# Moving the activation tiles against the weight buffers, modulo 512 bytes, stage by stage

## The reference

```
block 0:  proj = rmsnorm(x) @ nsa_w_in            # sparse attention, then memory attention
          x += concat(mix, cross) @ w_o[0]        # (256x1024) @ (1024x1024)        "wo0"
          x += swiglu(rmsnorm(x))                 # 1024 -> 2 x 2816 -> 1024        "f0"
block 1:  the same with the RWKV-7 recurrence as mixer; "wo1", "f1"
          x = rmsnorm(x)
block 2:  proj = rmsnorm(x) @ w_in_2              # spatial gating and forgetting attention
          x += rmsnorm(merged @ w_out_2)          # "wo2"
          x += rmsnorm(swiglu(rmsnorm(x)))        # "f2"
swiglu(h) = (silu(h @ w_gate) * (h @ w_up)) @ w_down     # hidden width 2816
```

## Time and profile before

| | us |
|---|---|
| median of 3 runs (1283.18 to 1285.41) | 1285.11 |
| the profiled execution | 1282.11 |
| its span, first to last instruction | 1280.3 |
| TensorE busy | 1204.6 (94%) |
| VectorE busy | 759.6 (59%) |
| ScalarE busy | 595.4 (47%) |
| mean granted TensorE clock | 0.966 |

### The profile page before, as it was taken

One profiled execution on the slowest core, in us unless ns is written; L12 is line 12 of the kernel. 1 busy time (PEld: TensorE's weight loads), 2 busy tenths in 40 slices (PEclk: granted clock), 3 DMA queues, 4 the chain that ended last, 5 costly groups with the idle time before them and its releaser, 6 DMA issues.

```text
span 1280.3 us, 24099 instructions
## 1 busy us (share of the span) xinstructions
PE 1204.6 (94%) x10320; PEld 1109.7 (87%) x10320; DVE 759.6 (59%) x1289; ACT 595.4 (47%) x1003; POOL 38.8 (3%) x44
## 2 busy tenths in 40 slices
PE   5999989999999998799799999999989988999997
PEld 4999878999988877798489999889988986999985
DVE  5555646666646677634566666465744575666644
ACT  4666545444435642232344444354328655444433
POOL 0000000000000102331000000000000000000000
PEclk9999989999999979899799999999989998999999
DMA  9822124867555431000259665537544343676651
GB/s 271 237 87 83 67 67 116 224 183 197 183 188 154 152 99 66 2 4 3 67 149 262 188 177 196 197 104 226 179 151 124 108 161 103 168 195 185 180 195 66
DMA packets 222693, 184.50 MB, mean 144 GB/s; under 512 B 19394, under 2 KB 208080, under 8 KB 222460
## 3 DMA queue, kind: packets, MB, share of 16 engines
q1 hardware_dynamic: 221386, 181.50, 47.6%
q10 hardware_dynamic: 1202, 1.47, 0.3%
HBM read 181.90 MB, written 1.05 MB: 143 GB/s over the span
## 4 chain that ended last, share of the span: by engine, by line
PE 83%; DVE 10%; ACT 4%; issue 1%; SPq 1%; DMA 1%; DVEq 0%; ACTq 0%
PE bank L776 23%; PE bank L777 22%; PE bank L778 22%; DVE w_lo L2027 2%; PE bank L1055 2%; PE bank L1273 1%; ACT w_hi L1580 1%; PE bank L1039 1%; PE bank L1249 1%; DMA ring<-in_nsa_w_in 1%; PE bank L1257 1%; PE bank L919 1%; SPq L713 1%; PE bank L923 1%; DVE act_lo L1997 1%
## 5 line engine op out<-in xcount | busy, mean ns | idle before, releaser
L2027 DVE TENSOR_TENSOR w_lo<-ring,w_hi 128x1024 fp32r<-128x1024 f32 x326 | 383.1, 1216 | 264.8 <-ACT w_hi L1580 264.6
L1580 ACT ACTIVATE w_hi<-ring 128x1024 fp32r<-128x1024 f32 x326 | 323.4, 1041 | 425.9 <-PE bank L778 407.4
L776 PE MATMUL bank<-act_hi,w_hi 128*128 128x256 f32 (+1 forms) x1512 | 428.0, 283 | 6.1 <-issue 3.4
L777 PE MATMUL bank<-act_lo,w_hi 128*128 128x256 f32 (+1 forms) x1512 | 424.6, 281 | 0.0
L778 PE MATMUL bank<-act_hi,w_lo 128*128 128x256 f32 (+1 forms) x1512 | 424.1, 280 | 0.0
L776 PEld LDWEIGHTS bank<-act_hi,w_hi 128*128 128x128 f32 (+1 forms) x1512 | 284.7, 188 | 10.7 <-issue 6.7
L777 PEld LDWEIGHTS bank<-act_lo,w_hi 128*128 128x128 f32 (+1 forms) x1512 | 284.6, 188 | 0.3
L778 PEld LDWEIGHTS bank<-act_hi,w_lo 128*128 128x128 f32 (+1 forms) x1512 | 283.9, 188 | 0.3
L776 PE MATMUL bank<-w_hi,act_hi 128*128 128x256 f32 (+1 forms) x448 | 141.0, 315 | 8.5 <-DVE act_lo L2503 4.2
L777 PE MATMUL bank<-w_lo,act_hi 128*128 128x256 f32 (+1 forms) x448 | 138.9, 310 | 0.0
L778 PE MATMUL bank<-w_hi,act_lo 128*128 128x256 f32 (+1 forms) x448 | 138.5, 309 | 0.0
(11 more groups left out here) (312 smaller groups left out, 1292.1 us busy)
## 6 DMA issues: line engine op xcount, KB each, us to landing
ring<-in_w_ffn_in SPq DMA_DIRECT2D x88, 512.0 KB, 5.2
ring<-in_w_in SPq DMA_DIRECT2D x28, 1024.0 KB, 5.3
ring<-in_w_ffn_out SPq DMA_DIRECT2D x22, 1024.0 KB, 4.9
ring<-in_rw_w_in SPq DMA_DIRECT2D x11, 1024.0 KB, 5.3
ring<-in_w_gate SPq DMA_DIRECT2D x22, 512.0 KB, 4.0
ring<-in_w_up SPq DMA_DIRECT2D x22, 512.0 KB, 5.2
ring<-in_w_down SPq DMA_DIRECT2D x11, 1024.0 KB, 4.9
ring<-in_w_o SPq DMA_DIRECT2D x8, 1024.0 KB, 4.9
```

Source lines behind the costliest of these rows:

```text
L776: pe.matmul(o, ahl[0], bhl[0], start=first, stop=False)
L777: pe.matmul(o, ahl[0], bhl[1], start=False, stop=False)
L1580: act.activation(w_hi[:, (m % SPLITS) * SLOT + lo:(m % SPLITS) * SLOT + hi], ring[:, r * SLOT + lo:r * SLOT + hi], copy).then_inc(tick(own ...
L2027: dve.tensor_tensor(w_lo[:, c], ring[:, r * SLOT + lo:r * SLOT + hi], w_hi[:, c].bitcast(F32), ALU.subtract).then_inc(tick(own, "lo_ready" ...
```

## The change

`act_hi` and `act_lo` become one region `act_pair` with 64 columns of room at its end. `home(shift)` gives the pair of views that begins `shift` columns further, and each stage has a shift of its own. `SHARED` is rounded up so that the arena lies at the same place modulo 512 bytes as the start of the region. `tt` moves with the home of `wo1`.

| stage | shift, columns | bytes past the weights' place | before |
|---|---|---|---|
| all others (`fm`) | 16 | 64 | 64 |
| `wo0` | 0 | 0 | 64 |
| `f0` | 8 | 32 | 64 |
| `wo1` | 48 | 192 | 64 |
| `f1` | 32 | 128 | 64 |
| `wo2` | 32 | 128 | 64 |
| `f2` | 64 | 256 | 64 |

```diff
-    act_hi = place("act_hi", KT * S, dtype=F32R)
-    ACT_LO = fixed_at[0]
-    act_lo = place("act_lo", KT * S, dtype=F32R)
+    LINE, ROOM, MIX1_HOME = 128, 64, 48
+    ACT_HI = fixed_at[0]
+    act_pair = place("act_pair", 2 * KT * S + ROOM, dtype=F32R)
+    ACT_LO = ACT_HI + KT * S
...
+    fixed_at[0] += (ACT_HI - fixed_at[0]) % LINE
     SHARED = fixed_at[0]
...
-    fm = (tiles(act_hi), tiles(act_lo))
+    def home(shift):
+
+        return tuple(tiles(act_pair[:, i * KT * S + shift:(i + 1) * KT * S + shift]) for i in range(2))
+
+    fm = home(16)
+    fm_of = {"wo0": home(0), "f0": home(8), "wo1": home(MIX1_HOME), "f1": home(32), "wo2": home(32), "f2": home(ROOM)}
...
-    tt = place("tt", 2 * H * CH, ACT_LO - SHARED).rearrange("p (r u t) -> p r u t", r=2, u=H)
+    tt = place("tt", 2 * H * CH, ACT_LO + MIX1_HOME - SHARED).rearrange("p (r u t) -> p r u t", r=2, u=H)
...
-                fm_unit(f"{tag}_in{j}", fm)
+                fm_unit(f"{tag}_in{j}", fm_of[tag])
...
-            row_unit("wo0_", j, 4, fm)
+            row_unit("wo0_", j, 4, fm_of["wo0"])
...
-        from_banks([(fm, lambda k: ("norm2", k))])
+        from_banks([(fm_of["f0"], lambda k: ("norm2", k))])
```

More of the change, by code:

```diff
@@ L1425, in _ @@
                 pe.wait_ge(sem("mix1_lo"), j + 1)
-            row_unit("wo1_", j, 4, fm)
+            row_unit("wo1_", j, 4, fm_of["wo1"])
         residual_to_fm(4, lambda i: evacuated("wo1_0", i))
@@ L1490, in _ @@
         for j in range(4):
-            row_unit("wo2_", j, 4, fm)
+            row_unit("wo2_", j, 4, fm_of["wo2"])
         residual_to_fm(4, lambda i: (sem("post_added"), i + 1))
@@ L1752, in _ @@
             step_end(s)
-        from_banks([(fm, None)])
+        from_banks([(fm_of["wo0"], None)])
         rows_ahead("wo0")
@@ L1799, in _ @@
         act.wait_ge(*filled("crT"))
-        act.activation(fm[0][:, 6:8, :], two("crT"), copy).then_inc(tick(own, "cross_hi"), 1)
+        act.activation(fm_of["wo1"][0][:, 6:8, :], two("crT"), copy).then_inc(tick(own, "cross_hi"), 1)
         def act_hop(hop, c):
@@ L1839, in _ @@
             act.wait_ge(sem("mix1_ready"), j + 1)
-            act.activation(fm[0][:, 2 * j:2 * j + 2, :], mix_fm[:, 2 * j:2 * j + 2, :], copy).then_inc(tick(own, "mix1_hi"), 1)
+            act.activation(fm_of["wo1"][0][:, 2 * j:2 * j + 2, :], mix_fm[:, 2 * j:2 * j + 2, :], copy).then_inc(tick(own, "mix1_hi"), 1)
         rows_ahead("wo1")
@@ L1843, in _ @@
         squares(4, x_tm)
-        from_banks([(fm, lambda k: ("norm2", 8 + k))])
+        from_banks([(fm_of["f1"], lambda k: ("norm2", 8 + k))])
         ahead("wo1_3")
@@ L1902, in _ @@
         ahead("gb3")
-        from_banks([(fm, None)])
+        from_banks([(fm_of["wo2"], None)])
         rows_ahead("wo2")
@@ L1907, in _ @@
         squares(8, x_tm)
-        from_banks([(fm, lambda k: ("ffn_pre_g_2", k))])
+        from_banks([(fm_of["f2"], lambda k: ("ffn_pre_g_2", k))])
         ahead("wo2_3")
@@ L2416, in _ @@
         dve.wait_ge(sem("cross_hi"), 1)
-        dve.tensor_tensor(fm[1][:, 6:8, :], two("crT"), fm[0][:, 6:8, :].bitcast(F32),
+        dve.tensor_tensor(fm_of["wo1"][1][:, 6:8, :], two("crT"), fm_of["wo1"][0][:, 6:8, :].bitcast(F32),
                           ALU.subtract).then_inc(freed(own, "crT"), 1)
@@ L2502, in _ @@
             ts = slice(2 * j, 2 * j + 2)
-            dve.tensor_tensor(fm[1][:, ts, :], mix_fm[:, ts, :], fm[0][:, ts, :].bitcast(F32),
+            dve.tensor_tensor(fm_of["wo1"][1][:, ts, :], mix_fm[:, ts, :], fm_of["wo1"][0][:, ts, :].bitcast(F32),
                               ALU.subtract).then_inc(tick(own, "mix1_lo"), 1)
```

## The result

The changed kernel takes 1286.5 us (median of 20 runs, 1283.0 to 1292.7), the kernel before 1280.1 us (20 runs, 1272.0 to 1289.7). The ratio is 1.0051, with a 95% interval of 1.0033 to 1.0069: slower by half a percent, where 1270 us and a gain were forecast. The stated range, 1251 to 1290, holds the time; the direction was the other one.

The account below looks back on a forecast made before the run. TensorE, busy 94% of the span, was taken as the bound through its matmul steps. 14.3 + 1.8 less about 0.6 gave 15.5 us off 1282.1, so 1266.6; plus 3.0 made 1269.6, stated as 1270, range 1251 to 1290.

Parts of the forecast that it names:

- What bounds the kernel, and what to read: Whole kernel: TensorE busy 94% of the span; the start-to-start matmul step counts, read from start times or window counts.
- First feed-forward products: f0, f1, f2: 3168 matmuls of 256 columns would step at 113.3 ns in place of 117.8, 14.3 us less.
- a sign of being wrong: Homes of f1 and f2: the prediction is wrong if 128 and 256 bytes are worse places than 64; no size given.
- the slow rival: f0, f1, f2 go to 120 ns or beyond: 1292 us at 120, 1313 at 127; chance 0.20.
- Two levels at one place: Matmuls with 256 columns: two stable levels, near 118 and 113 ns, can occur at one place, as in `sv0`.
- The other sign of being wrong: Feed-forward stages: the prediction is wrong if the level depends on how a stage is entered; no size given.
- Output projections: `wo0`, `wo1`, `wo2`, 96 matmuls of 512 columns each: 0.6 us less for each, 1.8 us in all.
- The rest of TensorE: 3456 matmuls and transposes outside `product`, whose operands move against each other: taken as 0, plus or minus 2 us.
- 510 to 630 us as long as now: The 120 us around the recurrence, holding 2418 matmuls and transposes, were to last as long as before.
- VectorE, ScalarE, weights in time: Splits and weight loads: no loss, 0 us; weights arrive in time; ScalarE's wait per unit falls from 3.03 to about 2.8 us.
- Nothing gives the gain back: Feed-forward units: 2.2 us of slack for the splits, of which a faster unit takes 0.2; loads keep up.
- The base: Starting time: profiled execution 1282.1 us, with 3.0 us added because the median of the runs shown was 1285.1.

Follow-up runs that it names:

- the second look: The changed kernel, unedited, profiled once more in a later set, where it took 1286.46 us, ratio 1.0034 to the kernel before.
- `f2_at_112`: Changed kernel with only the home of f2 moved, from 256 to 112 bytes: 1279.55 us, ratio 0.9975 to the kernel before.
- `all16`: Changed kernel with every home back at 64 bytes, in the new layout: 1282.4 us, ratio 1.0015 to the kernel before.
- `all16_same`: Changed kernel with every home at 64 bytes, timed again on one chip beside the changed kernel: 1286.23 us, ratio 1.0034 to the kernel before.
- `f28`: Changed kernel with f0, f1 and f2 at 112 bytes and all other homes at 64: 1272.6 us, ratio 0.9926 to the kernel before.
- `three_places`: Changed kernel with f0 at 0, f1 at 192 and f2 at 80 bytes, all other homes at 64: 1287.5 us in one look.
- `after`: First profiled look at the changed kernel, unedited; span 1282.2 us, median of its timed runs 1286.5 us.
- `best`: Changed kernel with f0, f1, f2 and projections of blocks 0 and 1 at 112 bytes, output projections at 0, block 2's projections at 64: 1266.2 us, ratio 0.9882 to the kernel before.

## Why the prediction was wrong, by its own steps

**What bounds the kernel, and what to read.** Right: the time is in the steps of the matmuls, and they follow the place. Each step was read from a count in a window, and the isolated matmul confirmed them to 0.1 ns. By the Trainium skill, "TensorE: Matmul & The Clock Gate", section "Step-by-step: what each phase is for", TensorE's two read ports are independent, loading the next weights takes no read bandwidth from the running matmul, and the step is the columns at 2.4 GHz plus about 2.5 ns. The isolated matmul, with nothing else at work, shows 113.3 to 120.0 ns by place where that gives 109, so for this form the trace does not agree.

**First feed-forward products: this is the step that failed.** It put f0, f1 and f2 at 113.3 ns, 14.3 us less, because two of the homes are farther from the weights' place than any in the trace and "a small push may be enough" to reach the lower level. They came to 116.6, 118.7 and 120.0: 1056 x (-1.1 + 0.6 + 2.3) / 1000 = +1.9 us. (In the second look f0 stayed at 117.8, which makes about +3 us.) The place is not a distance along which the loss shrinks. It repeats every 256 bytes, so f2's 256 bytes are the weights' own place again, whose 120 ns stood in the earlier trace rows. Modulo 512 was the diff's unit, and the prediction took it over without a row. The prediction named as a sign of being wrong that 128 and 256 bytes are worse places than 64, and they are. Where the low level came every time (30 isolated visits, 368 bytes included, and seven stages of the kernel) is 112 bytes, a place that neither kernel used. The bounds were right (113.2 to 120 ns holds all of it), and the slow rival named 120 ns and gave 1292, with a chance of 0.20; it came true for f2 alone, and the mean step of the three, 118.4 ns, stays under the 118.6 from which that rival was to decide. That the time went its way is partly luck: these steps are 1.9 us of the measured 6.4.

**Two levels at one place.** Right as a fact: f0 of the kernel before had 118 in three looks and 113 in one. But it was weighed too heavily: 3 of 24 isolated visits and 1 of 23 stages at 64 bytes. The rows it was read from, `sv0` and `fv`, are of another form, activations stationary, and forms have different rows. The other sign of being wrong, that the level depends on how a stage is entered, also came true: at 192 bytes a wait changed it. What in an entry chooses the level stays open.

**Output projections.** Right in sign, and `wo0` in size, by the very row it was taken from: 0.6, 0.4 and 0.1 us less, 1.1 in place of 1.8. `wo1` and `wo2` had no row. Their lower levels do not always come: `wo1` at 192 bytes ran at 233 in `f2_at_112`.

**The rest of TensorE, taken as 0 with plus or minus 2.** Mis-sized: up to +1.9 us in the two pieces above, near the edge of what was carried; by the timed runs of `all16` and `all16_same` +2.0 and +4.7, with intervals that hold 1.9. It is not a step of other matmuls but 0.9 us of waiting at f1's start and a longer stretch at half clock ahead of f2. Neither had a row. "510 to 630 us as long as now" holds (changed kernel, 2398 in place of 2418):

```profile
510.00:630.00 120.00, 100.43 (x2398) 90.33 (x2398) 60.65 (x123) 36.73 (x77) 27.01 (x36) 0.92 0.04 11
```

**VectorE, ScalarE, weights in time.** 0 was right for the splits. ScalarE's wait in a unit of f0 is 2.98 us, down from 3.03, for an f0 that gained 1.1 ns and not 4.5:

```profile
303.77 2.01 ACT L1587 ACTIVATE w_hi<-ring 128x1024 fp32r<-128x1024 f32 x2 [2.98 <-PE bank L785]
```

"Nothing gives the gain back" was not tested by the change. In `f28` the wait at f1's start is 1.4 us, but it is 0.7 to 1.1 with f1 at 64 bytes and 1.7 in `three_places`, where f1 ran faster only up to it; so at most some tenths of it are given back by the faster steps.

**The base.** 3.0 us were added because three runs had a median of 1285.1; 20 and 29 runs of that kernel gave 1280.1 and 1281.6. Its runs spread over 18 us, so three of them are no base for an effect of this size. From 1280.1 the same sum gives 1264.6.

**The account.** Steps of f0, f1, f2 +1.9, output projections -1.1, f1's start 0 (the look of `after` shows no such wait) to +1.0, the hand-over to f2 +1.0: +1.8 to +2.8 us of the measured 6.4 (first set) and 4.9 (last). The looks agree with it: the span is 1282.2 us for the changed kernel against 1280.1 to 1280.3 for the three looks of the kernel before that had all stages at 118. In the first set the changed kernel also ran at a mean clock of 0.9639. The clock of the kernel before in that set isn't on record; 17 of its runs in the next set had 0.9665, which would be worth 2.3 us at 0.9 us per 0.001, an estimate, and 1.2 of that is the half-speed stretch itself. Some 2 to 3.5 us of the medians stay without a place. Whether the moved constants and arena cause the longer stretch and the later load, and by what path, stays open: no kernel moved one of them alone. The four looks of the kernel before and nine of the ten at the new layout agree on the length of the stretch, counted with the half-speed piece at the start of `wo2` (10.2 us before, 13.6 after); `best`, the tenth, has 10.2 there in the new layout too.

## What to carry to other kernels

Before tiles are moved for their place, measure the form alone at all places, and visit each often enough to see all its levels: one short kernel gave the period and the best place, and `f28` (8 us faster than before) and `best` (15 us) followed from its table. Choose a place that has one level in every visit, not one that has a good one in some. Each form (which operand is stationary, how many columns) has its own best place, and a change that only moves addresses also moves whatever lies behind them, so run the new layout with the old distances as a control. Judge half a percent by a dozen runs beside their mean clock, not by three.

## What the runs showed that was not expected

- The step of an fp32r matmul with its own weight load depends on the distance of its two operands modulo 256 bytes: 113.3 to 120.0 ns for 256 columns, 226.7 to 234.2 for 512, with no other engine at work.
- The steps come in a few values, and a run of matmuls without a wait keeps the one it enters with: at 192 bytes 113.3 in 17 visits of 24 and 117.8 in 7, and in a stage of the kernel 113.3 up to a wait of 1.7 us and 117.8 after it.
- At half clock nothing is lost: 427 ns for 512 columns, against 233 at full clock in the same stage.
- The runs of one unchanged kernel lie between 1272 and 1292 us over all sets, and mostly follow the mean granted clock.
